# Both loads of the output weights issued by ScalarE instead of SyncE

## The reference, cut to what matters

```
def layer_output(x, o_branches, g_n, z_n, o_d, z_d, lam_init, lp):
    o_nsa = jnp.sum(o_branches * g_n[..., None], axis=2).reshape(B, T, NSA_WIDTH)
    o_d = (rms_norm(o_d, lp['diff_out_norm']) * (1.0 - lam_init)).reshape(B, T, DIFF_WIDTH)
    o = jnp.concatenate([o_nsa * jax.nn.silu(z_n), o_d * jax.nn.silu(z_d)], axis=-1)
    return x + o @ lp['w_out']

# new tokens, differential group: every past value row is read once
    v_all = jnp.concatenate([gather(cache_dv), v_d], axis=1)
    o_d = diff_attend(q_d, k_all, v_all, pos, jnp.arange(past + T), lam)
```

## Time and profile before

| | |
|---|---|
| median of 3 runs | 774.43 us (774.13 to 775.53) |
| the profiled execution | 775.79 us |
| its span, first to last instruction | 773.9 us |
| PE busy | 721.2 us, 93% of the span |
| DVE busy | 443.2 us, 57% |
| ACT busy | 200.5 us, 26% |
| mean DMA rate over the span | 282 GB/s |
| the chain that ended last | PE 53%, DVE 16%, issue 11%, SPq 8%, DMA 6% |

### The profile page before, as it was taken

How to read it: one execution, slowest core, us unless ns; L and a number is a source line. 1 busy time by engine, 2 the same in 40 slices (tenths; PEclk the granted TensorE clock), 3 DMA queues, 4 the chain that set the end, 5 groups by cost and what they waited for, 6 DMA issues and landing times.

```text
span 773.9 us, 14663 instructions
## 1 busy us (share of the span) xinstructions
PE 721.2 (93%) x4733; PEld 347.1 (45%) x4733; DVE 443.2 (57%) x953; ACT 200.5 (26%) x529; POOL 104.6 (14%) x198
## 2 busy tenths in 40 slices
PE   6999999999999999999999998888898887999996
PEld 2465544454545365444543562424344352433542
DVE  5351650715531456999768618777769656645373
ACT  3020011101200202311231215535456334433200
POOL 0000000000000010101001665622647000000000
PEclk9999999999999999999999999999999976999999
DMA  8797979899898999987978549999899849984621
GB/s 305 228 320 217 335 231 339 265 385 307 305 345 289 347 334 378 359 311 262 388 236 291 182 154 293 340 330 296 247 326 307 298 150 386 353 282 136 264 118 56
DMA packets 131686, 218.57 MB, mean 282 GB/s; under 512 B 17617, under 2 KB 55738, under 8 KB 130394
## 3 DMA queue, kind: packets, MB, share of 16 engines
q1 hardware_dynamic: 109514, 191.07, 72.1%
q0 software_dynamic: 7456, 14.80, 5.7%
q10 hardware_dynamic: 14640, 11.77, 4.9%
HBM read 211.71 MB, written 10.04 MB: 287 GB/s over the span
## 4 chain that ended last, share of the span: by engine, by line
PE 53%; DVE 16%; issue 11%; SPq 8%; DMA 6%; POOLq 2%; ACT 2%; POOL 1%; DVEq 0%; ACTq 0%
PE banks L634 13%; PE banks L662 9%; SPq L440 7%; PE banks L596 4%; PE banks L1043 4%; PE banks L675 4%; PE banks L762 3%; PE banks L1164 3%; DVE att L1884 3%; DMA proj<-in_cmp_cache 2%; PE banks L981 2%; PE banks L939 2%; PE banks L957 1%; DMA ring<-in_dv_cache 1%; POOLq L454 1%
## 5 line engine op out<-in xcount | busy, mean ns | idle before, releaser
L662 PE MATMUL banks<-ring,xt 128*128 128x512 f32 (+1 forms) x320 | 129.5, 558 | 0.0
L634 PE MATMUL banks<-proj,wide 128*64 128x256 f32 x896 | 98.2, 380 | 1.2 <-DMA proj<-in_cmp_cache 1.2
L1401 ACT ACTIVATE wide<-banks,att 128x384 f32<-128x384 f32 (+3 forms) x128 | 66.3, 523 | 124.5 <-DVE att L1884 121.2
L662 PEld LDWEIGHTS banks<-ring,xt 128*128 128x128 f32 x320 | 59.2, 190 | 63.9 <-issue 61.2
L458 POOL DMA_DIRECT2D ring<-in_sel_cache x143 | 74.8, 523 | 45.4 <-issue 39.1
L634 PEld LDWEIGHTS banks<-proj,wide 128*64 128x64 f32 x896 | 63.7, 137 | 38.0 <-DMA proj<-in_cmp_cache 5.6
L762 PE MATMUL banks<-ring,small 128*32 128x512 f32 x512 | 71.8, 641 | 6.4 <-DMA ring<-in_dv_cache 4.7
L1614 DVE TENSOR_SCALAR small<-small 128x510 f32<-128x510 f32 x8 | 3.4, 426 | 113.7 <-ACT small L1235 97.6
L675 PE MATMUL banks<-ring,small 128*32 128x512 f32 x512 | 61.6, 598 | 2.9 <-DMA ring<-in_dk_cache 2.9
L1883 DVE TENSOR_TENSOR banks<-banks,consts 128x256 f32<-128x256 f32 x64 | 27.3, 427 | 55.7 <-PE banks L939 55.3
L939 PE MATMUL banks<-proj 64*128 64x384 f32 (+7 forms) x256 | 53.5, 496 | 3.5 <-ACT wide L1401 3.5
(11 more groups left out here) (371 smaller groups left out, 883.8 us busy)
## 6 DMA issues: line engine op xcount, KB each, us to landing
ring<-in_dk_cache SPq DMA_DIRECT2D x256, 256.0 KB, 5.7
ring<-in_dv_cache SPq DMA_DIRECT2D x256, 256.0 KB, 5.4
proj<-in_cmp_cache SPq DMA_DIRECT2D x144, 128.0 KB, 2.9
ring<-in_w_in SPq DMA_DIRECT2D x6, 2048.0 KB, 12.5
proj<-in_cmp_cache ACTq DMA_DIRECT2D x80, 128.0 KB, 5.2
ring<-in_sel_cache POOLq DMA_DIRECT2D x143, 32.0 KB, 5.5
ring<-in_cmp_cache SPq DMA_DIRECT2D x32, 128.0 KB, 3.8
ring<-in_w_out SPq DMA_DIRECT2D x2, 2048.0 KB, 11.6
```

The lines of the kernel that those rows point to most:

```text
L634: last = mm(to, w1[:, kv, half, lp, :], rows[:, kv, g, lp, :, :, :], start=lp + half == 0, stop=lp == LP - 1 and half == 1, tile_position= ...
L662: last = mm(banks[:, 3 + n % 2, 0:width(c)], of, by, start=k == 0, stop=k == KC - 1)
L1401: last = A(e_slot(j, c)[:, 0:n], banks[:, 2 * (j % 2) + c, 0:n], ACT.Exp, bias=row_max[:, j % 4, c:c + 1], accum_out=row_sum[:, j % 4, c:c ...
```

## The change

SP no longer waits for `sel_valued` of the second batch and no longer issues `w_out`. ACT does both: in its loop over the rounds, in round `SEL_AT[1] + 5` = 42, behind its own work of that round, it waits for the semaphore and issues the two halves one behind the other. The bytes, the destinations and the semaphores that PE waits for are the same. The lines of everything behind move up by five to six.

```diff
-        SEL_MORE, W_OUT_AT = 26, V_EARLY + next(v for v in range(64) if v >= V_EARLY and V_ROUNDS[v - V_EARLY] > SEL_AT[1] + 4)
+        SEL_MORE = 26
@@ SyncE, in the loop over v
-                if v in (W_OUT_AT, W_OUT_AT + 2):
-                    c = (v - W_OUT_AT) // 2
-                    if c == 0:
-                        sp.wait_ge(s("sel_tensor"), sel_step(1, "sel_valued"))
-                    sp.dma_start(w_out[:, :, 512 * c:512 * c + 512], src["w_out"][:, :, 512 * c:512 * c + 512]).then_inc(s(f"w_out_in{c}"), 16)
                 load_v(v)
@@ ScalarE, in the loop over j, behind exps, scale_first and keep_b0
+                if j == SEL_AT[1] + 5:
+                    act.wait_ge(s("sel_tensor"), sel_step(1, "sel_valued"))
+                    for c in range(2):
+                        act.dma_start(w_out[:, :, 512 * c:512 * c + 512], src["w_out"][:, :, 512 * c:512 * c + 512]).then_inc(s(f"w_out_in{c}"), 16)
```

## The result

The changed kernel takes 772.71 us in the median of 20 runs (770.21 to 776.53), the kernel before 776.75 us beside it (20 runs, 771.68 to 781.13). The ratio is 0.9949, 95% interval 0.9932 to 0.9967: 0.51% faster, 4.0 us (2.6 to 5.3). 4.1 us, or 0.53%, had been predicted. The "before" of these runs is slower than the 774.43 that the prediction started from, so the ratio is what to compare.

A forecast was written before the change was run, and what follows sets the result against it. Bound: SyncE's 13.5 us wait before w_out held V44 while DMA idled, stalling PE for pages; PE bounds from 690. Profiled execution 775.79 - 4.1 - 0 = 771.7; against the median 774.43 - 4.1 = 770.3 us, range 768.5 to 773.6.

The forecast's parts named there:

- SP's wait held V44 and V45 through idle DMA time: SyncE's 13.5 us wait before w_out; without it two V steps go early and 5.4 us of transfers leave the saturated stretch.
- Both stalls for pages: PE's waits of 0.95 us before V44 and 1.71 us before V46 would go, 2.66 us together, the floor of the gain.
- DVE is what is late next: With pages on time, DVE's work in rounds 46 to 48 sets the pace, 4.06 us earlier at 654.69.
- The ceiling of 4.51 us: Most that DVE can come earlier at V47's matmuls: 0.95 + 3.11 + 0.45 us, with PE never late.
- 4.1 us for the stage: Gain taken for the rounds around V44 to V49, between the 2.66 us floor and the 4.51 us ceiling; chance 0.45.
- PE's way from L1023 through V46 to the end of the scores of round 48: PE at 2.4 GHz from 647.37 to 649.9, L1023 at half its 1.42 us, done before DVE is free at 650.6.
- The first rival: Clock stays 1.2 GHz over L1023, V46 and V47 as PE waits longer for DVE: only 2.7 us gained, 771.7; chance 0.24.
- ScalarE's issues cost nothing: ACT's two issues, 1.2 us from about 631.5, fit 1.25 us of idle time: cost 0 to 0.3 us, taken as 0.
- V47 near 646.5 by sharing or 651.7 in the worst order: Landing of V47: near 646.5 if queues take turns, 651.7 if w_out is served wholly ahead of the pages.
- Mixed queues: Rival: w_out and pages on two queues run at 331 GB/s, V52 lands at 670.2; 0.4 us gained, 774.0; chance 0.08.
- ScalarE was not held: Denies the rival that a full queue holds ACT in its second issue, up to 10.9 us: 4.5 us slower, 778.9; chance 0.07.
- as the rival took it: Rival on SyncE's moved issue: V44 and V45 do not start early, nothing is gained, 774.4; chance 0.04.

The follow-up runs named there:

- e2: Against the kernel before: SyncE still issues everything, but V44 and V45 ahead of the wait and both halves of w_out; ratio to before 0.9939, again 0.9954.
- e1: Against the changed kernel: ScalarE issues w_out, but SyncE still waits for the selected values in front of V44; ratio to before 1.0034.
- e7: Against the kernel before: SyncE issues V44 ahead of the wait, then the first half of w_out, V45, the second half, V46; ratio to before 0.9972.
- e10: Second run of the kernel of e6, the second half of w_out issued in round 50 against the changed kernel; ratio to before 0.9942.
- e3: Against the changed kernel: ScalarE issues w_out as eight DMAs of 512 KB instead of two of 2 MB; ratio to before 0.9948.
- e6: Against the changed kernel: ScalarE issues the second half of w_out in round 50 instead of round 42; ratio to before 0.9989.
- e11: Second run of the kernel of e7, only V44 ahead of SyncE's wait against the kernel before; ratio to before 0.9989.

## Why the prediction was right

- **SP's wait held V44 and V45 through idle DMA time: right.** They were issued at 619.8 and 626.5, in a trace that is 2.2 us late at V40 and V41 (618.27 and 623.70 against 616.09 and 621.50), so at 617.6 and 624.3 in before's time; 617.7 and 624 were forecast. e2 without the second queue and e1 with the wait show from both sides that this is the cause.
- **Both stalls for pages go, 2.66 us: right.** None is left in four traces of the two placements.
- **DVE is what is late next: right.** The timeline of DVE with `mask_max(48)` and `add_v(5)` in the changed kernel:

```profile
653.26 0.43 DVE L1882 TENSOR_TENSOR banks<-banks,consts 128x256 f32<-128x256 f32 x1 [0.88 <-PE banks L934]
...
655.29 0.75 DVE L1926 SCALAR_TENSOR_TENSOR xt<-banks,att,xt 128x512 f32<-128x512 f32 x1 [0.15 <-PE banks L757]
```

  Its idle times of 3.11 and 0.45 us became 0.88 and 0.15, where under 0.5 had been forecast for the first. The ceiling of 4.51 us less those 1.03 us, plus 0.1 (round 46 began 1.04 us earlier, counted from V43, not 0.95), gives the 3.58 us of the trace.
- **4.1 us for the stage, 3.58 measured.** The mis-sized term is PE's way from L1023 through V46 to the end of the scores of round 48, forecast at full clock with 2.5 us (647.4 to 649.9). It took 4.1, from 649.12 to DVE's start at 653.26, for two reasons. 0.7 us is a misreading in the prediction: it halved L1023's 1.42 us for full clock, but that row (from 648.32) already lay in the stretch at 1.00. After the change the same matmuls took 1.42 us again, at 1.00; at half clock the same four take 2.33 us (e7, at 648.58). The other 0.9 us is half clock that came back at 651.2: V46 took 1.65 us and the scores 0.80, most of it at 1.2 GHz. PE had been given 0.7 us of room ahead of DVE. The misreading used up the room, and the half clock became DVE's 0.88 us.
- **The first rival (low clock, 2.7 us) was half true.** Half clock came back for 3.4 us instead of 6.8, 2.1 us after PE's wait for the reciprocal had ended; that wait grew to 2.27 us, as the rival said. But the wait alone does not bring it. In e10, the changed kernel with half of w_out later, PE waited as long and the clock stayed at 1.00 until the end of the stage. PE and DVE there:

```profile
649.99 1.42 PE L1018 MATMUL banks<-xt,params 32*128 32x256 f32 x4 [2.18 <-DVE xt L1939]
651.70 1.07 PE L757 MATMUL banks<-ring,small 128*32 128x512 f32 x8
653.24 0.43 DVE L1882 TENSOR_TENSOR banks<-banks,consts 128x256 f32<-128x256 f32 x1
```

  PE took 3.2 us from L1018 to the end of the scores, 0.7 more than forecast, and DVE went through `mask_max(48)` and `add_v(5)` without idling. So at full clock DVE sets the pace, as predicted, though with 0.05 us to spare and not 0.7: the scores ended at 653.19. That trace's stage is 4.8 us shorter than before, a little above the ceiling of 4.51.
- **How near the number came is in part luck.** 4.0 us by the times (2.6 to 5.3) stands beside 4.1 forecast, but the two pairs of traces give 3.6 and about 3.5 us for the stage, each with a stretch of half clock that the 4.1 us had left out, and e10, without that stretch, gives 4.8.
- **ScalarE's issues cost nothing: right, for a reason better than the one given.** I had placed them behind L1412, in the idle 1.25 us; the sequencer issued them beside the engine's work.
- **V47 near 646.5 by sharing or 651.7 in the worst order.** V47 landed at 651.8 in a trace that runs 1.84 us later, 650.0 in before's time, between the two. V46 landed at 644.8, 642.9 in before's time, where about 641 had been given. The rates were about half each, the queues of the changed kernel from 638 to 650:

```profile
q10 hardware_dynamic: 1226, 2.48, 55.4%
q1 hardware_dynamic: 1185, 2.17, 49.0%
```

  The Trainium skill, "DMA: Bandwidth & Descriptors", section "Queues, rings and completion order", says that each DMA engine takes the queues in turn. From 638 on this trace agrees: 2.48 against 2.17 MB. V47 came 3.5 us later than by my estimate from it, and V46 1.9 us. The even shares began late: from 634 to 638, where V46's first page had been issued at 633.56, the queues read:

```profile
q10 hardware_dynamic: 631, 1.29, 94.9%
q1 hardware_dynamic: 22, 0.05, 2.9%
```

  Why the pages' transfers began 4 us after their issue is not shown.

- **The rivals that did not come.** Mixed queues ran at 386 to 387 GB/s, not 331. ScalarE was not held, even by eight issues (e3). The Trainium skill, "DMA: Bandwidth & Descriptors", section "Issuing engines are not separate DMA queues", says that another issuer saves only the time of the issue. Taken as the rival took it, for the whole worth of the change, it would have given 774.4, no gain, and the ratio of 0.9949 is against that. What it says of the issuer itself agrees with e2 and e1: ScalarE brought nothing, and the gain can be had on SP by order alone.

## What to carry to other kernels

Look for a semaphore wait in an issuer's stream that has nothing to do with what stands behind it: its price is the transfers that could have used the idle DMA time, not the wait. Reordering within one queue, urgent pages first, then the wait and the large load, gave here the same as another issuer; a second queue alone gives a large, patient load half of the rate and made this kernel slower. Measure a change of half a percent in its stage, from one fixed instruction to another, since a single execution is moved by more than the change elsewhere: V42 begins at 623.64 in e7 and at 632.49 in e11, which are one kernel, and a stretch of half clock in the tail alone cost 1.7 us.

## What the runs showed of the hardware that was not expected

- ScalarE's sequencer issues a DMA while the engine still computes: both issues began within the engine's rows from 632.42 to 633.50, and the second ended at 633.78.
- Two hardware queues of equal pieces (2 KB) share nearly evenly, 55% and 49% of the engines' time, at an unreduced 386 GB/s.
- SP's first issue behind both halves of w_out took 3.1 us in e2 and 4.0 in the second trace of before; eight issues that together carry 4.2 MB were not held on ScalarE. It seems that an issuer is held when it adds to such a queue, not when it fills it; the limit itself was not measured.
- One stretch of 3.4 us at 1.2 GHz cost the same kernel 1.2 us of its stage (e6 against e10).
